# A ninth gather buffer instead of a second weight piece buffer in the last layer

## The reference

```
h    = rms_norm(x) * (1 + sc1) + sh1
proj = h @ w_in
fox  = forgetting_attention(...)      # 8 heads: softmax with a learned decay, causal
sb   = stick_breaking_attention(...)  # 8 heads: log_sigmoid(z) plus a suffix sum of log_sigmoid(-z), exp, causal
x    = x + gt1 * (concat(rms_norm(fox), rms_norm(sb)) @ w_out)
h2   = rms_norm(x) * (1 + sc2) + sh2
x    = x + gt2 * peer_layer(h2)
```

```
query      = h2 @ w_query                        # 2 x 128 per head
sub_scores = query . sub_keys                    # 128 keys for each half
experts    = the 16 best of the 16 x 16 sums of the best of each half
gates      = softmax(their scores)
act        = gelu(h2 . expert_down[experts]) * gates
out        = sum over the 16 of act * expert_up[experts]
```

## Time and profile before

| | |
|---|---|
| median of 3 runs | 2853.65 us (2849.81 to 2857.81) |
| profiled execution | 2848.87 us, its span 2847.1 us |
| granted TensorE clock, mean | 0.892 of 2.4 GHz |
| busy: PE, DVE, ACT, POOL | 78%, 53%, 31%, 21% of the span |
| DMA: software queue (gathers) | 556.90 MB |
| DMA: SP's and ACT's queues | 381.17 MB and 8.75 MB |
| first gather of the paired layer issued | 1382.0 us |
| last one issued | 2811.6 us |

### The profile page before, as it was taken

How to read it: one execution, slowest core, us unless ns; L and a number is a source line. 1 busy time by engine, 2 the same in 40 slices (tenths; PEclk the granted TensorE clock), 3 DMA queues, 4 the chain that set the end, 5 groups by cost and what they waited for, 6 DMA issues and landing times.

```text
span 2847.1 us, 30061 instructions
## 1 busy us (share of the span) xinstructions
PE 2217.2 (78%) x10252; PEld 1009.6 (35%) x10252; DVE 1505.1 (53%) x3429; ACT 882.8 (31%) x1857; POOL 607.1 (21%) x588
## 2 busy tenths in 40 slices
PE   5997999888778775999977667986679876665554
PEld 2455444532222222755643223432335322321110
DVE  3997844400000003201678666787667677677764
ACT  3105301110101002311277323873238543232221
POOL 1000000100000001000244333443333343344442
PEclk9999999899999997999998789987989778888777
DMA  9785455399999998021699999999998899999996
GB/s 373 280 187 148 178 193 228 135 393 410 416 415 415 418 422 313 18 81 67 240 410 420 391 422 399 388 412 414 420 422 321 362 407 412 421 421 422 421 421 290
DMA packets 155969, 948.46 MB, mean 333 GB/s; under 512 B 18522, under 2 KB 50312, under 8 KB 65982
## 3 DMA queue, kind: packets, MB, share of 16 engines
q0 software_dynamic: 78704, 556.90, 47.8%
q1 hardware_dynamic: 68224, 381.17, 34.6%
q10 hardware_dynamic: 8910, 8.75, 0.9%
HBM read 914.99 MB, written 31.77 MB: 333 GB/s over the span
## 4 chain that ended last, share of the span: by engine, by line
PE 47%; DMA 31%; DVE 12%; ACT 5%; issue 4%; POOL 1%; SPq 0%; ACTq 0%; DVEq 0%; POOLq 0%
PE bank L2054 16%; DMA ring<-in_expert_pair,ids 13%; DMA ring<-in_w_exp_up 12%; PE bank L2688 8%; PE bank L2060 6%; PE bank L2344 6%; DMA arena_h<-in_expert_pair,ids 5%; DVE ring L2003 3%; DVE arena_h L2003 1%; DMA ring<-in_w_mod 1%; ACT arena_w L1383 1%; PE bank L2699 1%; PE bank L2633 1%; PE bank L2529 1%; PE bank L2487 1%
## 5 line engine op out<-in xcount | busy, mean ns | idle before, releaser
L2688 PE MATMUL bank<-ring,arena_w 128*32 128x512 f32 x1436 | 558.9, 724 | 246.2 <-ACT arena_w L1383 246.0
L942 POOL DMA_INDIRECT ring<-in_expert_pair,ids x359 | 394.0, 1097 | 849.4 <-PE bank L2688 482.2
L2003 DVE CUSTOM_DVE_ANT_0 ring<-ring 128x1024 f32<-128x1024 f32 x359 | 435.3, 1225 | 176.3 <-DMA ring<-in_expert_pair,ids 149.9
L2054 PE MATMUL bank<-arena_h,ring 128*128 128x128 f32 (+2 forms) x1264 | 365.0, 449 | 3.2 <-ACT arena_h L1183 3.2
L2688 PE MATMUL bank<-arena_h,arena_w 128*32 128x512 f32 x468 | 268.1, 744 | 111.7 <-ACT arena_w L1383 111.6
L2344 PE MATMUL bank<-ring,arena_h 128*64 128x512 f32 x1056 | 262.2, 654 | 76.1 <-DMA ring<-in_w_exp_up 71.4
L2688 PEld LDWEIGHTS bank<-ring,arena_w 128*32 128x32 f32 x1436 | 98.4, 122 | 486.9 <-ACT arena_w L1383 337.2
L2054 PEld LDWEIGHTS bank<-arena_h,ring 128*128 128x128 f32 x1264 | 204.3, 196 | 158.3 <-issue 122.9
L1718 DVE TENSOR_TENSOR arena_q<-arena_q,bank 128x256 f32<-128x256 f32 x32 | 13.5, 421 | 465.5 <-ACT arena_q L1120 465.5
L1381 ACT ACTIVATE arena_w<-arena_w 128x2 f32<-128x2 f32 x256 | 51.9, 203 | 663.3 <-DVE arena_w L2003 662.7
L942 POOL DMA_INDIRECT arena_h<-in_expert_pair,ids x117 | 130.1, 1112 | 232.5 <-PE bank L2688 194.6
(11 more groups left out here) (471 smaller groups left out, 3011.0 us busy)
## 6 DMA issues: line engine op xcount, KB each, us to landing
ring<-in_w_exp_gate SPq DMA_DIRECT2D x33, 2048.0 KB, 19.1
ring<-in_w_exp_up SPq DMA_DIRECT2D x33, 2048.0 KB, 23.4
...
```

The lines of the kernel that those rows point to most:

```text
L942: pool.indirect_dma_start(pair[pair_of(m)], None, A["expert_pair_2"], bass.IndirectOffsetOnAxis(ap=ids[n % 2][:, r:r + 1], axis=0)).then_i ...
L2003: dve.tensor_tensor_reduce(buf, buf, h2_q[r % 4], 1.0, 0.0, ALU.mult, ALU.add, dots[:, r:r + 1]).then_inc(dots_done, 1)
L2054: mm = pe.matmul(dst, w[:, c, at], rhs[:, c, :], start=(c == 0), stop=(c == chunks - 1))
L2688: mm = pe.matmul(bank[4 + half][at, :], sel_q[:, n % 2, k0 + j, :], pair[pair_of(m + j)][:, D + 512 * half:D + 512 * half + 512], start=Fa ...
```

## The change

The paired layer has nine gather buffers for its first three tiles and twelve for the last. The ninth is the second half of `hold_a`. For that, weight pieces have one buffer, the first half: SP issues piece i when PE has used piece i - 1. The product with `w_out` is cut into four steps of one piece each, in parts 32, 34, 36 and 38. The second norm moves from part 36 to 38, the transposes from 39 to 41, and the queries stand in parts 43, 46, 49, 51, 54, 57, 59 and 62. The scratch in `hold_a` is two deep throughout. Gather 14 still waits for the fifth query step (`2 * EARLY` is 14, as `EARLY + PAIRS_0 - 1` was).

```diff
-PAIRS_0, PAIRS = 8, 11
+PAIRS_0, PAIRS = 9, 12
...
-        stick_x = [[spare[:, P * i:P * i + P] for i in range(3)], [view(hold_a, T * i, T) for i in range(3)]]
-        stick_y = [[spare[:, P * (3 + i):P * (4 + i)] for i in range(3)], [view(hold_a, T * (3 + i), T) for i in range(5)]]
+        stick_x = [[spare[:, P * i:P * i + P] for i in range(3)], [view(hold_a, T * i, T) for i in range(2)]]
+        stick_y = [[spare[:, P * (3 + i):P * (4 + i)] for i in range(3)], [view(hold_a, T * (2 + i), T) for i in range(2)]]
...
-        fprob = [[view(pair_last, P * i, P) for i in range(3)], [view(hold_a, T * i, T) for i in range(3)]]
-        fprobT = [[view(pair_last, P * (3 + i), P) for i in range(2)], [view(hold_a, T * (3 + i), T) for i in range(2)]]
+        fprob = [[view(pair_last, P * i, P) for i in range(3)], [view(hold_a, T * i, T) for i in range(2)]]
+        fprobT = [[view(pair_last, P * (3 + i), P) for i in range(2)], [view(hold_a, T * (2 + i), T) for i in range(2)]]
...
         pair += [arena_h[:, 2 * D * i:2 * D * i + 2 * D] for i in range(2)]
+        pair += [hold_a[:, 2 * D:4 * D]]
         pair += [arena_v[:, 2 * D * i:2 * D * i + 2 * D] for i in range(1, 4)]
         FIRST = (TT - 1) * H * K16
-        EARLY = PAIRS_0 - 1
+        EARLY = PAIRS_0 - 2
...
-            at = hold_a[:, 2 * D * (i % 2):2 * D * (i % 2) + 2 * D]
-            turn = 16 * ((t - 1) * PIECES // 2 + i // 2 + 1)
-            there = (slab_in[slot2(S_WQ + 2)], loaded2(S_WQ + 2) + turn) if i % 2 == 0 else (wo_b_in, turn)
+            at = hold_a[:, 0:2 * D]
+            there = (slab_in[slot2(S_WQ + 2)], loaded2(S_WQ + 2) + 16 * ((t - 1) * PIECES + i + 1))
...
-        LATER = {ST_NORM: 30, ST_TURN: 31, ST_OUT: 32, ST_OUT + 1: 36, ST_COLS: 39}
-        LATER.update({ST_QUERY + h: at for h, at in enumerate((41, 44, 48, 51, 54, 57, 60, 62))})
+        LATER = {ST_NORM: 30, ST_TURN: 31, ST_OUT: 32, ST_OUT + 1: 34, ST_OUT + 2: 36, ST_OUT + 3: 38, ST_COLS: 41}
+        LATER.update({ST_QUERY + h: at for h, at in enumerate((43, 46, 49, 51, 54, 57, 59, 62))})
...
-                    if 2 <= i < 6:
-                        sp.wait_ge(wo_pe, wo_used(t, i - 2))
-                    elif i >= 6:
-                        sp.wait_ge(q_pe, wq_used(t, i - 6))
-                    sp.dma_start(dst, src).then_inc(there, 16)
-                    if i == 1:
+                    if 1 <= i < 5:
+                        sp.wait_ge(wo_pe, wo_used(t, i - 1))
+                    elif i >= 5:
+                        sp.wait_ge(q_pe, wq_used(t, i - 5))
+                    sp.dma_start(hold_a[:, 0:2 * D], src).then_inc(there, 16)
+                    if i == 0:
...
-                if n >= 3:
-                    act.wait_ge(sbr_pe, n - 2)
+                if n >= len(stick_x[part]):
+                    act.wait_ge(sbr_pe, n + 1 - len(stick_x[part]))
...
-            def attended_b(t, j):
-                for half in range(2):
-                    w, there, _ = piece(t, 2 * j + half)
-                    pe.wait_ge(*there)
-                    for c in range(4):
-                        mm = pe.matmul(bank[WO_BANKS[1][j]][:, :], mixT2[1][:, 4 * half + c, :], w[:, c, :],
-                                       start=(half == 0 and c == 0), stop=(half == 1 and c == 3))
-                    mm.then_inc(wo_pe, 1)
+            def attended_b(t, q):
+                j, half = q // 2, q % 2
+                w, there, _ = piece(t, q)
+                pe.wait_ge(*there)
+                for c in range(4):
+                    mm = pe.matmul(bank[WO_BANKS[1][j]][:, :], mixT2[1][:, 4 * half + c, :], w[:, c, :],
+                                   start=(half == 0 and c == 0), stop=(half == 1 and c == 3))
+                mm.then_inc(wo_pe, 1)
```

26 lines of the change are left out of this document (12 added, 14 removed).

## The result

The changed kernel took 2881.98 us (median of 4 runs, 2876.32 to 2884.65) beside 2852.03 us for the kernel before (4 runs): ratio 1.0081, 95% interval 1.0054 to 1.0107. A repeat on another chip, beside 29 runs of before, gave 1.0091 (1.0056 to 1.0125). It is slower, by 23 to 26 us by these ratios; the medians themselves lie 30 and 23 us apart. Forecast was 2846.3, with a range up to 2860.

What follows compares the result with a forecast made beforehand. The prediction took the last layer to be bound by DMA gathers, with 47.2 us lost in dips. Terms of -15.3, +5.9 and +2 summed to -7.4 us, giving 2846.3 us, range 2836 to 2860.

Steps and rivals of the forecast that it cites:

- term 2: One weight piece buffer: PE's product chain lengthens and DVE waits in the norm; +5.9 us, bounds -2.5 and 14.4.
- rival D: TensorE's clock drops for matmuls behind PE's waits for pieces; if a third counts, sum -0.1 us, 2853.6; chance 0.05.
- Term 1: Ninth gather buffer: one gather more moved at each DMA dip; -15.3 us, bounds nothing and 20.3.
- Rival C: The ninth gather buffer gains nothing, consumers being the bound after each dip; +7.9 to +13 us; chance 0.10.
- Term 3: Scratch two deep: ACT's first step on a stick head waits for PE's sums two heads back; +2 us.
- Rival A: Waits for pieces don't reach DVE and the ninth buffer's gain stays; -15.8 us, 2837.9; chance 0.25.
- Rival B: Chain of pieces: longer landings delay the last product in three tiles; +8.6 us at landings of 11.3; chance 0.14.

Runs made afterwards that it cites:

- e3: The changed kernel with the ninth gather buffer taken out again (8 buffers, 11 in the last tile); ratio to the kernel before 1.0132.
- e7: The kernel before with only the new plan (product in four steps, norm at 38) and one piece buffer; ratio to before 1.0079.
- e8: The changed kernel with 11 matmuls of zeros (9.7 us) on PE ahead of products 2 to 4 of a tile; ratio to before 1.0095.
- e13: The changed kernel with half-size pieces in two buffers, 2.6 us of zero matmuls before products 2 to 4, scratch three deep, norm at 39; ratio to before 0.9968.
- e15: e13 run once more, unchanged; ratio to before 0.9980.

## Why the prediction was wrong

The step that failed is term 2, one piece buffer at +5.9 us. Alone it measures +22.5 us (16 to 29). One of its inputs was right: pieces land after 9.1 us. The price of a stall came out right by luck. With stalls of 21.8, 21.7 and 21.9 us from the norm's first instruction to the next dot, 1.4 + 0.81 x (stall - 9.5) gives 11.4, 11.3 and 11.4 us; the three dips lost 10.2, 11.6 and 11.2. But 2.49 us were to come off each for the ninth buffer, and with eight buffers, where nothing comes off, the price is too low: the stalls are 19.7, 18.4 and 20.2 us in e3 and 19.2, 19.0 and 18.9 in e7, for which it gives 28 and 27 us in all, and the norms lost 35.6 and 38.5. The price is 2.4 and 3.7 us a dip too low there, about what the ninth buffer was to take off. What was wrong is the wait, 1.7, 6.4 and 6.3 us in the forecast and 12.3, 12.2 and 12.4 in the trace:

- The products. I took 3.7 us for each, from products that PE ran into without a wait. Behind a wait for a piece they take 5.3 to 6.7 us. In tile 1 the four sum to 22.4 us for 14.8, 7.6 more, while the rest of the chain is 26.3 us for the 27.3 of three landings. So the chain is 48.7, 46.4 and 45.7 us for 42.1.
- DVE came to its norm 35.1, 33.0 and 32.0 us after the first product began, for 39.0, 34.3 and 34.4. Moving a step by two parts did not move it by two parts' worth of gathers.

For tile 1: 1.7 + 6.6 + 3.9 = 12.2. For tiles 2 and 3 the same sum gives 12.0 and 12.3.

The mechanism of the first point stood in the prediction as rival D, priced for the sums behind each wait and only for a third of them. Its place was the products themselves, where it lengthens a chain that already was too long. The Trainium skill ("TensorE: Matmul & The Clock Gate", HAM oscillation) says that matmuls behind a pause for a transfer start at the low clock. The traces agree: a product takes 3.60 us where e8 fills the waits, and 5.3 to 6.7 us behind waits of 4.4 to 8.4 us in after.

The query pieces were rightly put at nothing, though PE waits more often for them than I counted: twelve times, 35.8 us in all, where I had six waits of 3.1 us. No window of 25 us loses anything between 1675 and 1775 us, between 2050 and 2150 or from 2425 on, where the queries stand.

**Term 1** (-15.3) was right in its size: 12 to 17 us by time. Its count of one gather for each dip is not borne out place by place (see the ninth buffer above). Rival C is refuted. Its upper end was wrong by the way: without the 2.49 us the three norms come to +7.0 and with term 3 to +9.0, not +13.

**Term 3** (+2, bounds 0 to 4.5) was too small by time. The mechanism was right, the count was not: I charged one late head in tile 3 and half of one in tile 2. In tile 3 ACT waits for the sums before six of the eight heads:

```profile
  PE bank L2546: 16.4, 6
```

The scratch costs 5.4 to 13.7 us by time alone (1.0 in the tail part), and 8 to 11 (10 to 16) when taken out of the changed kernel.

**The sum.** -14.5 (ninth buffer), +22.5 (piece and plan) and +9.4 (scratch) give +17 us; measured are +23 and +26, with intervals of 7 to 10 us on each side. The first of these is itself a difference to the changed kernel, so what the sum checks is whether piece, plan and scratch make up e3: 31.9 us of its 37.7. They do within their scatter.

Rival A is refuted: the pieces do reach DVE. Rival B has the right place with the wrong price, since landings stayed at 9.1 us and it was the products that grew. The sign of being wrong that I named, a dip of more than 7 us at the norms, is what came: 10.2, 11.6 and 11.2.

**The dip at 2250 us** had no term. It is 11.1 us in before and 11.3 in its copy, and absent in both profiles of after. In before it follows a stretch of 23.2 us in which PE is busy without a gap, at a granted clock of 0.50 of 2.4 GHz, that is 1.2. POOL waits up to 8.6 us for PE's sums, and the DMA engines fall idle. The stretch in before, then windows of e13, and of e15, which is the same kernel:

```profile
2243.30:2266.50 23.20, 23.20 (x57) 9.73 (x54) 13.37 (x32) 12.46 (x24) 4.44 (x4) 0.50 0.76 304
```

```profile
2275.00:2300.00 25.00, 22.05 (x150) 11.22 (x151) 20.34 (x54) 19.89 (x38) 13.41 (x11) 1.00 1.01 421
```

```profile
2250.00:2275.00 25.00, 21.62 (x60) 9.23 (x56) 16.19 (x38) 12.80 (x25) 6.72 (x6) 0.61 1.01 412
2275.00:2300.00 25.00, 23.36 (x140) 10.52 (x138) 17.42 (x45) 16.80 (x33) 10.89 (x10) 0.91 0.79 290
```

The fox heads of tile 3 stand there. A pair of records of their scores (L2488 in before, L2486 in after) takes 1.12 us at full clock and 2.07 at the low one:

```profile
2246.29 2.07 PE L2488 MATMUL bank<-arena_w,ident 8*128 8x512 f32 x2
...
2257.03 2.07 PE L2488 MATMUL bank<-arena_w,ident 8*128 8x512 f32 x2
```

```profile
2258.68 1.12 PE L2486 MATMUL bank<-arena_w,ident 8*128 8x512 f32 x2
```

In before the clock falls soon after a wait of 3.2 us for ACT, which ends at 2241.9. Over all 19 profiles the lost time between 2250 and 2325 us follows the number of such heads: 8.3 to 11.3 us in the five with two of them, 2.2 to 6.6 in the six with one, 1.5 at most in the eight with none. e13 has none and e15 two, so it depends on the execution and not only on the program. So both profiles of after are spared 11 us that those of before lose, by no term of the forecast; from two profiles of each it isn't known whether that is luck. It also lies in every comparison of single profiles above.

One thing stays open: the scratch alone costs 9.4 us by time but 1.0 by its profile, and the changed kernel 23 to 26 for 14 to 20. The profile is one execution of four to twelve. No run tells whether a changed program makes the stages ahead of the first gather slower, or whether that is scatter.
